# Expert routing in a hybrid decoder step: the tokens' choices brought to all partitions through a DRAM scratch instead of by four products and four copies

## What is computed

```python
def _moe(h, router, wg, wu, wd):
    logits = jnp.einsum('btd,de->bte', h, router).astype(jnp.float32)
    top_v, top_i = lax.top_k(logits, TOP_K)
    probs = jax.nn.softmax(top_v, axis=-1)
    combine = jnp.sum(jax.nn.one_hot(top_i, N_EXPERTS, dtype=jnp.float32) * probs[..., None], axis=-2)
    y = jnp.zeros(h.shape[:-1] + (wd.shape[-1],), h.dtype)
    for e in range(N_EXPERTS):
        y = y + combine[..., e:e + 1].astype(h.dtype) * _swiglu(h, wg[e], wu[e], wd[e])
    return y
```

## Time and profile before

| | |
|---|---|
| device time, median of 3 runs | 1492.08 us (1491.62 to 1494.45) |
| the profiled execution's own device time | 1497.22 us |
| its span in the profile | 1495.4 us |
| PE busy | 1457.7 us, 97% of the span |
| DVE, ACT, POOL busy | 751.8, 345.9 and 78.6 us |
| granted TensorE clock, mean | 0.994 |
| bytes moved | 302.12 MB, mean 202 GB/s |

### The profile page before, as it was taken

How to read it: one execution, slowest core, us unless ns; L and a number is a source line. 1 busy time by engine, 2 the same in 40 slices (tenths; PEclk the granted TensorE clock), 3 DMA queues, 4 the chain that set the end, 5 groups by cost and what they waited for, 6 DMA issues and landing times.

```text
span 1495.4 us, 40378 instructions
## 1 busy us (share of the span) xinstructions
PE 1457.7 (97%) x17741; PEld 1246.0 (83%) x17741; DVE 751.8 (50%) x1672; ACT 345.9 (23%) x879; POOL 78.6 (5%) x104
## 2 busy tenths in 40 slices
PE   8999999999999999999999999999999899999997
PEld 6899877887999999998899867878978787788754
DVE  6546666636765656566357467545741221221123
ACT  2334324123112222133243232231220000000001
POOL 1200010200000000001100100200020000000000
PEclk9999999999999999999999999999999999999999
DMA  8335353113644444348435352116979988999992
GB/s 343 140 116 193 144 164 107 64 45 97 232 147 164 142 169 143 113 153 274 184 127 222 119 152 87 46 48 204 379 284 349 366 328 298 349 369 361 376 389 98
DMA packets 65644, 302.12 MB, mean 202 GB/s; under 512 B 22583, under 2 KB 24359, under 8 KB 38975
## 3 DMA queue, kind: packets, MB, share of 16 engines
q1 hardware_dynamic: 50392, 268.10, 49.5%
q0 software_dynamic: 4256, 20.41, 3.7%
q10 hardware_dynamic: 10823, 11.05, 2.8%
HBM read 279.05 MB, written 19.30 MB: 200 GB/s over the span
## 4 chain that ended last, share of the span: by engine, by line
PE 90%; DVE 4%; DMA 3%; issue 2%; ACT 1%; SPq 0%; DVEq 0%; ACTq 0%
PE ps L2112 15%; PE ps L1913 12%; PE ps L1265 10%; PE ps L1713 9%; PE ps L2035 7%; PE ps L1720 5%; PE ps L1214 4%; PE ps L1825 4%; PE ps L2009 3%; DMA ring<-in_mix 2%; PE ps L1227 2%; PE ps L1569 2%; PE ps L1787 2%; PE ps L1946 2%; PE ps L1545 1%
## 5 line engine op out<-in xcount | busy, mean ns | idle before, releaser
L1713 PE MATMUL ps<-xn,ring 128*128 128x288 f32 x576 | 155.1, 413 | 0.3 <-ACT gate L2500 0.3
L1713 PEld LDWEIGHTS ps<-xn,ring 128*128 128x128 f32 x576 | 105.8, 190 | 36.7 <-issue 9.4
L2112 PE MATMUL ps<-arena 128*128 128x144 f32 x1028 | 133.4, 285 | 0.9 <-DVE arena L3700 0.9
L2112 PEld LDWEIGHTS ps<-arena 128*128 128x128 f32 x1028 | 129.3, 189 | 1.0 <-issue 1.0
L1913 PE MATMUL ps<-y_ml,arena 128*64 128x96 f32 (+4 forms) x2688 | 113.4, 246 | 9.4 <-issue 9.3
L1913 PEld LDWEIGHTS ps<-y_ml,arena 128*64 128x64 f32 x2688 | 110.8, 138 | 13.2 <-issue 13.2
L2035 PE MATMUL ps<-arena,mixed 128*32 128x256 f32 x2024 | 111.8, 380 | 0.0
L2035 PEld LDWEIGHTS ps<-arena,mixed 128*32 128x32 f32 x2024 | 66.5, 110 | 41.3 <-issue 0.5
L3624 DVE TENSOR_TENSOR mixed<-ps,mixed 128x96 f32<-128x96 f32 (+4 forms) x66 | 16.8, 254 | 138.6 <-PE ps L1913 138.3
L1913 PEld LDWEIGHTS ps<-y_ml,ring 128*64 128x64 f32 x1536 | 65.4, 141 | 9.2 <-issue 9.2
L1913 PE MATMUL ps<-y_ml,ring 128*64 128x96 f32 (+4 forms) x1536 | 69.2, 250 | 3.4 <-issue 3.2
(11 more groups left out here) (604 smaller groups left out, 2484.1 us busy)
## 6 DMA issues: line engine op xcount, KB each, us to landing
arena<-in_egu SPq DMA_DIRECT2D x56, 1024.0 KB, 7.2
ring<-in_mix SPq DMA_DIRECT2D x46, 1024.0 KB, 5.1
arena<-in_edown SPq DMA_DIRECT2D x40, 1024.0 KB, 7.2
ring<-in_mix SPq DMA_DIRECT2D x48, 768.0 KB, 4.3
ring<-in_egu SPq DMA_DIRECT2D x32, 1024.0 KB, 7.4
ring<-in_gu SPq DMA_DIRECT2D x14, 1024.0 KB, 4.9
arena<-in_gu SPq DMA_DIRECT2D x8, 1024.0 KB, 5.3
arena<-in_C POOLq DMA_DIRECT2D x2, 2048.0 KB, 8.2
```

The costliest lines, as they stand in the source:

```text
L1713: last = mm(ps[:, bank, 0:T], ring[:, s, P * k:P * k + P], xn[:, k, :], start=(k == 0), stop=(k == KT - 1))
L2112: last = mm(ps[:, dense_bank(side, product), 0:HALF], left, right, start=(k == 0 and product in (1, 2, 5)), stop=(k == n - 1), skip_group_ ...
```

## The change

Four products on PE and two copies each on ACT and DVE go. In their place POOL, behind its six scatters, writes the four rows to a small DRAM scratch `choice_rows`, waits for that transfer, and reads them back with a source that repeats for all 128 partitions, into `chosen`. DVE waits for this transfer (`ld_chosen`) where it waited for the copies. PE's wait for the copies ahead of `turn_slots` goes too. The constant `sel` (512 columns) is no longer needed, so that the load of `con` is shorter.

```diff
-               ("g4", 2), ("bmask", 8), ("bmask2", 8), ("bsel", NH * SB), ("sel", 512), ("sel_s", 128)):
+               ("g4", 2), ("bmask", 8), ("bmask2", 8), ("bsel", NH * SB), ("sel_s", 128)):
...
-            def broadcast_choices():
-
-                pe.wait_ge(*rt_cr(0))
-                for v, bank in enumerate((7, 4, 5, 6)):
-                    mm(ps[:, bank, 0:T], con[0:4, CON["sel"] + P * v:CON["sel"] + P * v + P], gate_rows[0:4, 0, :],
-                       start=True, stop=True).then_inc(rt_bc.sem, 1)
-
...
-                    if f == 3 and first:
-                        broadcast_choices()
...
-                    if p == 0:
-                        pe.wait_ge(rt_cha.sem, 2)
-                        pe.wait_ge(rt_chd.sem, 2)
-                    else:
+                    if p > 0:
                         pe.wait_ge(sc_e.sem, p * KT)
...
-                    if f == 3 and first:
-                        for v, bank in ((0, 7), (2, 5)):
-                            act.wait_ge(rt_bc.sem, v + 1)
-                            A(chosen[:, v, :], ps[:, bank, 0:T], ACT.Copy).then_inc(rt_cha.sem, 1)
...
                         extra_passes()
-                        for v, bank in ((1, 4), (3, 6)):
-                            dve.wait_ge(rt_bc.sem, v + 1)
-                            dve.tensor_copy(chosen[:, v, :], ps[:, bank, 0:T]).then_inc(rt_chd.sem, 1)
...
                         if first:
-                            dve.wait_ge(rt_cha.sem, 2)
-                            dve.wait_ge(rt_chd.sem, 2)
+                            dve.wait_ge(ld_chosen.sem, 16)
                         pick_places(p, blocks)
...
+            pool.wait_ge(*rt_cr(0))
+            pool.dma_start(choice_rows, gate_rows[0:4, 0, :]).then_inc(choices_out.sem, 16)
+            pool.wait_ge(choices_out.sem, 16)
+            pool.dma_start(chosen[:, :, :], choice_rows.unsqueeze(0).broadcast_to([P, 4, T])).then_inc(ld_chosen.sem, 16)
```

More of the change, by code:

```diff
@@ L184, in shape_constants @@
     put("fold8", r[:, None] % TS == np.arange(2 * NH)[None, :])
-    put("sel", np.repeat(np.eye(NH), P, 1))
     put("lead", (r % TS == 0)[:, None] * np.ones((P, P)))
@@ L771, in build @@
         xt = con[:, CON["swap"]:CON["swap"] + 3 * D].rearrange("p (i d) -> p i d", i=3)
-        assert CON["swap"] + 3 * D <= CON["sel"]
+        assert CON["swap"] + 3 * D <= CON["sel_s"]
         xg = flat(y_ml)[:, 0:KT * MB].rearrange("p (k n) -> p k n", k=KT)
@@ L795, in build @@
         sample_rows = nc.dram_tensor("sample_rows", (NH, NH + 1, TS), F32, kind="Internal").ap()
+        choice_rows = nc.dram_tensor("choice_rows", (4, T), F32, kind="Internal").ap()
         old_scales = nc.dram_tensor("old_scales", (SB * NH,), F32, kind="Internal").ap()
@@ L953, in build @@
         rt_zero = sig("route_zero")
-        rt_ex, rt_bc, rt_cha, rt_chd = sig("rt_ex"), sig("rt_bc"), sig("chosen_scalar"), sig("chosen_vector")
+        rt_ex, choices_out, ld_chosen = sig("rt_ex"), sig("choices_written"), sig("chosen_loaded")
         xt_p, xt_a = sig("xt_p"), sig("xt_a")
```

## The result

The changed kernel takes 1503.28 us (median of 6 runs, 1500.59 to 1509.11), the kernel before beside it 1491.85 us (6 runs, 1486.1 to 1494.45). The ratio is 1.0091, with a 95% interval of 1.0073 to 1.0109: slower by 11 to 16 us, where 2.8 us of gain were forecast. The profiled execution spans 1499.3 us.

What follows compares the result with a forecast made beforehand. PE, busy 97% of the span, was taken to bound the kernel. Products 2.13 plus clock 1.82 less PE's 1.15 us wait gave 2.8 us gain, from 1492.1 to 1489.3 us; range 1487.0 to 1494.0.

Steps and rivals of the forecast that it cites:

- Rival D: Late landing of `chosen` in pass 0 makes the kernel slower, 1499 to 1501 us, deciding from 1129.85; chance 0.12.
- the formula: On PE in pass 0, tile 8 starts at the later of 1129.96 and the landing of `chosen` plus 4.1 us.
- Step 2: POOL's write of four rows on q0 takes 3.2 us, landing just behind the scatter at 1119.1; bounds 1118.4 and 1121.8.
- far bound: For POOL's write, the 13.1 us of `old_scales`, made of single elements, giving a landing at 1129.0.
- Step 3: POOL's read to 128 partitions, issued at about 1119.3, takes 7.7 us; `chosen` lands at 1127.0, bounds 1126.0 and 1129.8.
- The deadline: DVE is ready for `pick_places` at 1124.9, tile 8 could start at 1129.96; nothing is lost for landings up to 1125.9.
- The products: The four products on PE between tiles 3 and 4 of pass 0 go, winning 2.13 us on the chain.
- The clock: Without the products PE keeps full clock in tile 4 of pass 0, winning 1.82 us, lower end 0.
- The costs at nothing: Copies on ACT and DVE, PE's wait before `turn_slots`, the shorter `con` load and the added traffic each count 0.

Runs made afterwards that it cites:

- read-alone run: Changed kernel with the scratch written once, with zeros, ahead of the scatters, so only the read stands behind them: 1494.88 us, ratio 1.0020 to the kernel before.
- idle transfers: Kernel before, products and copies kept, plus the same write and read into an unused part of `xn`, with no early wait: 1493.46 us, ratio 1.0009.
- ACT's queue: Changed kernel with the write issued by ACT behind its silu of tile 3 and the read behind that of tile 5: 1503.81 us, ratio 1.0037.
- with the wait: Kernel before with the unused write and read added, and DVE waiting for their landing ahead of `pick_places` of pass 0: 1505.59 us, ratio 1.0082.
- scatters last: Changed kernel with POOL's write and read ahead of its six scatters: one execution, 1499.96 us, beside a kernel before of 1497.86 us.

## Why the prediction was wrong

**The cover, not only the size.** Rival D had the right mechanism and the formula was right: tile 8 starts 4.1 us after the landing (1132.9 + 4.1 = 1137.0, measured 1137.06). D had 0.12. (Its point for a loss beyond 0.2%, 1133.7, should have been 1129.85 + 3.0 = 1132.85.) What failed are three terms of the steps that led to it.

**Step 2, the write at 3.2 us (bounds to 5.9), measured 9.7, and 9.6 to 10.1 in three other runs.** I took the scatter on q0 for over at 1118.2 and counted from there. The write's completion came in with the end of the scatter (q0 still moves 0.22 MB between 1121 and 1123.2), and the scatter itself ends later than I had it: 9.4 us after POOL's last issue in the read-alone run, which has no write behind it, against 6.5 us in the profile of before (1111.99 to 1118.5). Only the far bound, 13.1 us, held; I had set it aside because those were single elements. What stands on the queue decided here, not the size of the transfer.

**Step 3, the read at 7.7, measured 9.3,** and 9.1 to 10.9 over the eight profiles named above. Mis-sized by 1.4 to 3.2 us, for it is released together with the weight loads. The estimate of 3.4 us that the Trainium skill's fit gives for these bytes ("DMA: Bandwidth & Descriptors", "Anatomy of one DMA — SWDGE (gpsimd) path") is 1.2 us below the quiet duration of 4.6 us; beside weight loads the read took about three times the estimate.

**The deadline.** This is the largest. Counted from the start of tile 0 (1100.36 before, 1101.91 with the change), the measured landing stands at 1131.35 on the forecast's clock, 4.4 us late, and the formula then gives tile 8 at 1135.45. That is 1.5 us later than before, not 11 to 16. The rest comes from where PE could have been: I dated everything on one execution, in which PE lost some 5 us in tile 2 in gaps without a releaser, and then ran at half clock. That execution took 5.1 us more than the median. I wrote that the gain should be the same in the median, but the gaps fall between the scatter's start, which sets when `chosen` can land, and tile 5, which sets when it is wanted. A run without them has that much less cover. Five of the thirteen profiles of this study have no such gaps, that of the change among them. From the profile of the idle transfers, which is a kernel before with its products (its chain, start us, us, what):

```profile
1102.34 5.50 PE ps L1915 x128
1107.84 0.43 PE ps L1902 x3
1108.27 5.43 PE ps L1915 x128
1113.70 2.13 PE ps L1909 x8
1115.84 15.66 PE ps L1915 x376
```

Tiles 2 and 3 take 5.43 us together there, and tile 7's product on DVE, behind which PE begins tile 8, comes early:

```profile
1126.66 0.26 DVE L3627 TENSOR_TENSOR mixed<-ps,mixed 128x96 f32<-128x96 f32 x1 [1.12 <-PE ps L1915]
```

So tile 8 starts about 24.2 us after tile 0 there, 33.6 in the profile of before and 35.15 with the change: 10.9 us lost against a kernel before without gaps, and 2.6 by the clock behind the wait, 13.5 in all. The chain of tiles 2 and 3 in the profile of before:

```profile
1106.30 1.68 PE ps L1913 x31
1107.97 0.44 issue
1108.42 0.39 PE ps L1913 x3
...
1113.23 0.23 issue
```

It needs 13.1 us for them, from 1106.30 to 1119.40. The right question for an added wait was how early its consumer can be, not when it was in one trace.

The gaps go with the chip as far as the record tells. The four profiles on the second chip, where the kernel before takes 1492.03 us, have none, and all seven on the two others (1496.19 and 1497.86) have them. On those two, four of the six profiles with gaps in tile 2 were faster than the median of their own runs, so a comparison with the median would not have shown the gaps there; it was a sign only for the profile of before. And the chips with gaps give an added wait more cover: with ACT's queue, DVE waited 8.6 us there, and the ratio was 1.0037.

**The products, 2.13 us:** right as a size. They are gone, and with no transfers the kernel is 0.7 and 1.4 parts in a thousand faster, 1.0 and 2.1 us, both with 0 in the interval.

**The clock, 1.82 us:** not a fixed cost of the products. In the profile with idle transfers they run and the clock stays at full speed; in that with the wait it falls right behind them (windows of the first, around its products, then of the second):

```profile
1113.70:1115.84 2.14, 2.14 (x11) 1.41 (x12) 1.60 (x9) 0.82 (x2) 0.87 (x2) 1.00 0.98 354
1115.84:1119.50 3.66, 3.66 (x90) 3.66 (x92) 0.93 (x3) 0.25 (x1) 0.00 (x0) 1.00 1.02 416
...
1110.80:1113.90 3.10, 3.10 (x34) 2.32 (x32) 2.28 (x10) 0.82 (x2) 0.98 (x2) 0.99 1.00 395
1113.90:1117.60 3.70, 3.70 (x56) 3.70 (x54) 0.00 (x0) 0.25 (x1) 0.00 (x0) 0.54 1.00 406
```

So the same four products are followed by half clock in two executions (this one and that of before) and not in a third. In all ten profiles without the products the clock stays at 1.00 through tiles 4 and 5. So the fall is worth up to 1.8 us in some executions; the forecast counted it whole. What lets the third execution keep its clock is open, and that the four-partition products alone cause the fall was not tried by itself.

**The costs at nothing** held as far as they were tried: the traffic costs nothing that can be told (1.0009, 0.9994 to 1.0024). The copies, PE's dropped wait and the shorter load of `con` were not tried alone; together with the products they are within the 1.0 and 2.1 us above.

**What stayed right:** that PE bounds the stage and that SP follows it. The PE microseconds lost in pass 0 were lost at the end (12.7 us added up, 11 to 16 measured).

## What to carry to other kernels

A transfer put in the place of work that an engine does in 2 us must be covered for as long as write, completion and read take in a busy stretch, here 18 to 21 us in six profiles (9.7 and 9.3 with the change). So the consumer's position matters more than the transfer: with `pick_places` behind PE's last tile no loss could be told. Before a small transfer is put on a queue, look what is ahead of it there, and who else is released by the same completion. Date a deadline by the fastest execution of the consumer, not by one profile: take several, on more than one chip, above all when the one at hand is slower than the median.

## What the runs showed of the hardware that was not expected

- A write of 4.5 KB took 4.7 and 4.8 us with an empty queue and 9.6 to 10.1 us right behind 2.36 MB of indirect scatter on the same queue. That scatter alone ended 9.4 us after its last issue (read alone), so such a write lands with it. From ACT's queue, as the scatter ended, at most 5.3 us.
- A read of 4.6 KB of DRAM repeated to 128 partitions took 4.6 us alone (one execution) and 9.1 to 10.9 us beside weight loads (eight), on POOL's queue or ACT's alike.
- PE's gaps of 0.3 to 1.0 us after every few matmuls (some 5 us in all in the profile of before) come while the scatters run: with the scatters last, they stand in tile 6, while POOL issues these, from 1120.71 to 1125.96, instead of in tile 2. Five profiles have none although they scatter during tile 2: that of the change and the four on the second chip (its repetition, the idle transfers without and with the wait, the read alone). Why these are spared is open; the chip is the one difference that the record shows for the four.
- PE stood 12.2 us and then ran its first 5.35 us at half clock, 2.6 us more for three tiles: this stall cost more than its length.
